# An encoder layer in one program: where the gelu projections, the first recurrence product and the normalisation of the probabilities stand in the order of work

## What is computed

```python
proj = x @ w_in + b_in
u_lru, g_lru, q, k, v, gate_lru, gate_attn = split(proj)
u = depthwise_conv(u_lru)                       # 4 taps, 1280 channels
h = scan(u, forward gates) + scan(u, backward gates)
    # r, i = sigmoid(block_diag(u) + b);  a = exp(8 r log_sigmoid(lam));  h_t = a h_{t-1} + sqrt(1-a^2) i u
y_lru  = (h * gelu(g_lru)) @ w_lru_out
y_attn = windowed_gqa(q, k, v) @ w_attn_out     # 8 heads, 2 KV heads, blocks of 128, +-128 keys, a sink logit
mix = (sigmoid(gate_lru) * y_lru + sigmoid(gate_attn) * y_attn) @ w_o + b_o
x = layer_norm(alpha * x + mix)
hu = depthwise_conv(x @ w_up + b_up)            # 3 taps
val, gt = split(hu)
out = layer_norm(alpha * x + (gelu(gt) * val) @ w_down + b_down)
```

## Time and profile before

| | us |
|---|---|
| median of 3 runs | 2766.47 (2766.07 to 2767.06) |
| the profiled execution, its own time | 2770.9 |
| its span, first to last instruction | 2769.1 |
| PE busy | 2671.8 (96%) |
| DVE / ACT / POOL busy | 1506.4 / 753.4 / 654.1 |
| long sequence: recurrence, attention, merge | 11 to 331, 331 to 741, 741 to 1039 |
| short sequence: recurrence, attention, merge | 1834 to 1998, 1998 to 2201, 2201 to 2356 |

### The profile page before, as it was taken

How to read it: one execution, slowest core, us unless ns; L and a number is a source line. 1 busy time by engine, 2 the same in 40 slices (tenths; PEclk the granted TensorE clock), 3 DMA queues, 4 the chain that set the end, 5 groups by cost and what they waited for, 6 DMA issues and landing times.

```text
span 2769.1 us, 32046 instructions
## 1 busy us (share of the span) xinstructions
PE 2671.8 (96%) x11898; PEld 2202.5 (80%) x11898; DVE 1506.4 (54%) x1800; ACT 753.4 (27%) x1033; POOL 654.1 (24%) x332
## 2 busy tenths in 40 slices
PE   8997999999899999999999999989999999999998
PEld 6886788888678877888888888878788778888886
DVE  7899864334313657745445464667742314644445
ACT  4565713313210022010101011148831211211112
POOL 3554531231133612334343433310000000000000
PEclk9998999999899999999999999999999999999999
DMA  6565654444686833434343534357756794544554
GB/s 232 183 204 185 213 193 160 172 157 159 262 353 231 301 125 137 137 137 153 136 179 128 188 124 161 132 215 235 244 186 228 256 343 159 205 183 182 192 201 168
DMA packets 174272, 535.67 MB, mean 193 GB/s; under 512 B 13863, under 2 KB 40743, under 8 KB 172112
## 3 DMA queue, kind: packets, MB, share of 16 engines
q1 hardware_dynamic: 116992, 430.94, 43.1%
q10 hardware_dynamic: 57168, 103.21, 10.5%
HBM read 310.99 MB, written 214.19 MB: 190 GB/s over the span
## 4 chain that ended last, share of the span: by engine, by line
PE 82%; DVE 9%; DMA 4%; ACT 2%; issue 1%; POOL 1%; ACTq 0%; SPq 0%; DVEq 0%; POOLq 0%
PE ps L857 48%; PE ps L1176 12%; PE ps L1003 8%; PE ps L1097 4%; PE ps L907 3%; PE ps L1036 2%; PE ps L986 2%; DMA gate_in<-gate_dram 1%; DMA W<-w_split 1%; PE ps L1023 1%; PE ps L910 1%; PE ps L1165 1%; DVE tau L1750 1%; DMA al_dram<-AOL 0%; DMA w_split<-W 0%
## 5 line engine op out<-in xcount | busy, mean ns | idle before, releaser
L857 PE MATMUL ps<-XH,W 128*128 128x512 f32 x4224 | 1208.2, 392 | 24.9 <-DVE XL L1695 11.6
L857 PEld LDWEIGHTS ps<-XH,W 128*128 128x128 f32 x4224 | 798.0, 189 | 202.1 <-issue 18.4
L857 PE MATMUL ps<-XL,W 128*128 128x512 f32 x2112 | 712.1, 391 | 0.0
L857 PEld LDWEIGHTS ps<-XL,W 128*128 128x128 f32 x2112 | 399.2, 189 | 83.1
L1176 PE MATMUL ps<-W,HH 128*128 128x512 f32 x1152 | 310.4, 389 | 1.7 <-DVE HL L2006 1.5
L1176 PEld LDWEIGHTS ps<-W,HH 128*128 128x128 f32 x1152 | 216.1, 188 | 47.3 <-DVE HL L2006 1.9
L741 POOL TENSOR_SCALAR W<-raw 128x1024 fp32r<-128x1024 f32 (+2 forms) x72 | 95.4, 1325 | 587.2 <-PE ps L857 277.6
L1003 PE MATMUL ps<-XH,W 128*128 128x512 f32 x672 | 216.4, 393 | 0.0
L807 POOL TENSOR_SCALAR W<-raw 128x1024 fp32r<-128x1024 f32 x72 | 87.4, 1213 | 535.3 <-PE ps L857 224.9
L742 POOL TENSOR_TENSOR W<-raw,W 128x1024 fp32r<-128x1024 f32 (+2 forms) x72 | 200.5, 2785 | 6.0
L808 POOL TENSOR_TENSOR W<-raw,W 128x1024 fp32r<-128x1024 f32 x72 | 191.9, 2666 | 6.0
(11 more groups left out here) (203 smaller groups left out, 3360.6 us busy)
## 6 DMA issues: line engine op xcount, KB each, us to landing
w_split<-W SPq DMA_DIRECT2D x131, 1024.0 KB, 6.4
W<-w_split SPq DMA_DIRECT2D x130, 1024.0 KB, 6.9
raw<-w_mlp SPq DMA_DIRECT2D x72, 512.0 KB, 4.9
raw<-w_qkv_mix SPq DMA_DIRECT2D x28, 512.0 KB, 3.9
w_split<-W SPq DMA_DIRECT2D x8, 1280.0 KB, 12.0
W<-w_split SPq DMA_DIRECT2D x8, 1280.0 KB, 7.7
gate_dram<-mix_out ACTq DMA_DIRECT2D x16, 512.0 KB, 2.7
gate_in<-gate_dram ACTq DMA_DIRECT2D x16, 512.0 KB, 6.2
```

Source lines behind the costliest of these rows:

```text
L857: last = nc.tensor.matmul(bank(group, c), lhs(wl, k), rhs(xl, k, c), start=(k == 0 and n == 0), stop=(k == nk - 1 and n == 2))
```

## The change

It has four parts.

1. **The gelu projections of the second half.** `order_lru` puts `g(1,1)` ahead of gate block (1,1), `g(1,2)` ahead of (1,2) and `g(1,3)` ahead of (1,3). The table `taken_behind` keeps ACT's order as it was, apart from `g(1,0)`, which ACT takes between its two squares of block (1,0). The numbers p of the projections, and so their PSUM groups, are the same.
2. **SP's order at gate slabs (q = 0).** The load of a gate slab stands ahead of the moves of the block before; at (h, 1) `stack_second` and a save too.
3. **The first recurrence product as a fill.** Output 0 of the `w_lru_out` product goes to banks 2-3 and is issued in pieces in the last blocks of kv = 1 (`Y_FILL`): contraction tiles 0-1, 2-4, 5-7 for the long sequence, 0-3, 4-7 for the short. Output 1 follows whole, in banks 4-5. `YR` is loaded by SP for both sequences; gates 0 and 1 are loaded at the start of kv = 1 and their sigmoids are ahead of ACT's wait for the attention's stores. Buffers are laid out anew for it.
4. **Normalisation.** DVE runs `normalise(n+1)` in `tails_of(n)`, ahead of its subtraction on the block's output; DVE no longer waits at the end of the long sequence's attention.

```diff
-                     ("gates", 1, 0), ("g", 1, 0), ("u", 1, 2),
-                     ("gates", 1, 1), ("g", 1, 1), ("u", 1, 3),
-                     ("gates", 1, 2), ("g", 1, 2), ("g", 1, REST_TILE),
-                     ("gates", 1, 3), ("g", 1, 3)]
+                     ("gates", 1, 0), ("g", 1, 0), ("u", 1, 2), ("g", 1, 1),
+                     ("gates", 1, 1), ("u", 1, 3), ("g", 1, 2),
+                     ("gates", 1, 2), ("g", 1, REST_TILE), ("g", 1, 3),
+                     ("gates", 1, 3)]
+        taken_behind = {(0, 0): (("g", 0, 0), ("u", 0, 2), ("g", 0, REST_TILE)), (0, 1): (("g", 0, 1), ("u", 0, 3)),
+                        (0, 2): (("g", 0, 2), ("u", 1, 0)), (1, 0): (("u", 1, 2),),
+                        (1, 1): (("g", 1, 1), ("u", 1, 3)), (1, 2): (("g", 1, 2), ("g", 1, REST_TILE))}
...
+        def lru_group(m):
+
+            return (1, 2)[m] if m < 2 else m % 2
+
+        Y_FILL = ({(6, 1): range(0, 2), (7, 0): range(2, 5), (7, 1): range(5, 8)},
+                  {(3, 0): range(0, 4), (3, 1): range(4, 8)})
...
                 for n, (kind, h, jj) in enumerate(order_lru):
-                    if kind == "gates" and jj:
-                        moves_of_block(0, T, h, jj - 1)
                     if kind == "gates":
                         load(n, n % 2, A["w_gate"][HALF * h + jj, :, :], GATEW)
...
+                    if kind == "gates" and jj > 1:
+                        moves_of_block(0, T, h, jj - 1)
+                    if kind == "gates" and jj == 1:
+                        stack_second(0, T, h)
...
+                    if kind == "gates" and jj == 1:
+                        moves_of_block(0, T, h, 0)
...
-                    if q:
-                        for dst, src in zip(YR[q], (yh_dram, yl_dram)):
-                            sp.dma_start(dst[:, :, 0:T].bitcast(F32), src[q][BLOCKS:RT, :, :].rearrange("k p t -> p k t")).then_inc(y_in[4][q], 16)
+                    if q == 0:
+                        sp.wait_ge(scores_full[q], GROUP * (T // P) * KV)
+                    for dst, src in zip(YR[q], (yh_dram, yl_dram)):
+                        sp.dma_start(dst[:, :, 0:T].bitcast(F32), src[q][BLOCKS:RT, :, :].rearrange("k p t -> p k t")).then_inc(y_in[4][q], 16)
...
+                    def y_fill(n, side):
+
+                        part = Y_FILL[q].get((n, side))
+                        if part is None or kv == 0:
+                            return
+                        if part.start == 0:
+                            pe.wait_ge(mix_taken[q], KD * 2)
+                            slab_in(q, "y_lru", 0)
+                        y_product(0, part)
...
                             mixture_gates(n, 0)
+                            y_fill(n, 0)
                             if n + 1 < nb:
                                 scores(n + 1, (2, 3))
                             turn(n)
                             mixture_gates(n, 1)
+                            y_fill(n, 1)
                             mix_values(n)
...
-                    for m in range(2):
-                        slab_in(q, "y_lru", m)
-                        y_product(m, range(BLOCKS))
-                    for m in range(2):
-                        y_product(m, range(BLOCKS, RT)).then_inc(slab_done, 1)
-                    for m in range(2, KD):
-                        pe.wait_ge(prod_taken[q], m + 1)
+                    y_product(0, range(filled, RT)).then_inc(slab_done, 1)
+                    for m in range(1, KD):
+                        if m == 1:
+                            pe.wait_ge(pt_split[q], KV * pt_before(nb, nb))
+                        elif m == 2:
+                            pe.wait_ge(scores_out[q], GROUP * nb * KV)
+                        else:
+                            pe.wait_ge(prod_taken[q], m + (0 if m == 3 else 1))
                         slab_in(q, "y_lru", m)
                         y_product(m, range(RT)).then_inc(slab_done, 1)
...
+                            if d:
+                                between()
...
+                            decays(h, jj, [side(r, jj, T) for r in sig[0:2]],
+                                   (lambda: take("g", 1, 0)) if (h, jj) == (1, 0) else (lambda: None))
...
-                                for e in behind_gates(h, jj):
+                                for e in taken_behind[h, jj]:
                                     take(*e)
...
-                        if q and kv:
-
+                        if kv:
+
+                            if q == 0:
+                                act.wait_ge(qkv_split[q], 5 * KV)
                             for m in range(2):
                                 act.wait_ge(mix_stored[m][q], 16)
                                 load_gate(m)
...
+                    sigmoid(0)
+                    sigmoid(1)
                     for k in range(3):
                         act.wait_ge(ao_stored[k][q], 32 * ((KV * nb - k + 2) // 3))
...
+                            if n + 1 < nb:
+                                normalise(n + 1)
                             dve.wait_ge(ao_head[q], blk + 1)
...
-                    end_phase(dve, end_of(q, "attn"))
+                    end_phase(dve, end_of(q, "attn"), wait=q > 0)
```

More of the change, by code:

```diff
@@ L274, in build @@
         for k in range(6):
-            part(turn + 64 * 1024 + k * 8192 if k < 2 else at_h + (k - 2) * 8192)
+            part(at_h + k * 8192)
             wo[0].append(place(f"wo{k}", [P, 2, D_MODEL], F32R))
@@ L509, in feature_tile @@
             return BLOCKS + h if jj == REST_TILE else HALF * h + jj
-        def behind_gates(h, jj):
-            at = slab_at[("gates", h, jj)] + 1
-            out = []
-            while at < len(order_lru) and order_lru[at][0] != "gates":
-                out.append(order_lru[at])
-                at += 1
-            return out
         phases = ["lru", "attn", "mlp"]
@@ L940, in _, with y_rhs, y_ready_of, y_product @@
                     per_block = 2 // len(chunks(T))
+                    def y_rhs(t, kk, c):
+                        if kk < BLOCKS:
+                            return x_rhs(t, kk, c)
+                        return YR[q][t][:, kk - BLOCKS, c * CH:(c + 1) * CH]
+                    def y_ready_of(kk):
+                        if kk % 2 == 0:
+                            pe.wait_ge(y_in[kk // 2][q], 64 if kk < BLOCKS else 32)
+                    def y_product(m, part):
+                        return product(lru_group(m), T, RT, slab_lhs(slot_of(q, "y_lru", m)), y_rhs, y_ready_of, part)
+                    def y_fill(n, side):
[6 more added lines that the diff above has]
+                        y_product(0, part)
+                    filled = max(part.stop for part in Y_FILL[q].values())
                     for kv in range(KV):
@@ L1505, in _, with sigmoid @@
                         store(nb - 1)
+                    def sigmoid(i):
+                        act.wait_ge(gate_loaded[i % 2][q], 16 * (i // 2 + 1))
+                        A1(gate_in[q][i % 2][:, 0:T], gate_in[q][i % 2][:, 0:T], ACT.Sigmoid).then_inc(gate_ready[q], 1)
+                    sigmoid(0)
+                    sigmoid(1)
                     for k in range(3):
```

56 lines of the change are left out of this document (19 added, 37 removed).

## The result

The changed kernel takes 2795.57 us (median of 4 runs, 2794.46 to 2796.43) where the kernel before takes 2766.76 (2766.07 to 2767.79): a ratio of 1.0103, with a 95% interval from 1.0091 to 1.0115. It is 28.8 us slower. The forecast was 2769.3, the range 2749 to 2783. The profiled executions differ by less, 2794.5 - 2769.1 = 25.4 us of span, because the one of before was 4.1 above its median and the other 0.9.

A forecast was written before the change was run, and what follows sets the result against it. PE, busy 96% of the span, was taken as the bound, with only 97 us idle and lost clock winnable. Terms -2.2 + 6.2 + 13.6 - 10.8 - 4 = +2.8 us gave 2769.3 us, range 2749 to 2783.

The forecast's parts named there:

- Part 2, -2.2: Long recurrence: SP's earlier gate load removes 1.1 us POOL waits at (0,2) and (0,3), 2.2 us faster; bounds -2.2 and 0.
- PE's next gate block is far enough behind to cover it: Long recurrence, block (0,1): moves come some 4 us later than before, but PE would not be delayed.
- Part 1, long sequence, +6.2: Long recurrence: the 10.9 us won are given back in waits and clock losses, 6.2 us slower; bounds -1.0 and +8.
- The three waits for the gelu: Long recurrence: PE waits for ACT ahead of g(1,2), g(1,3) and the second attention product; steps give 3.5, 3.5, 6.3 us.
- a chain on DVE that the change leaves alone: Long recurrence: scans of block (1,0) still done at 246.4, so ACT's first sigmoid of block (1,1) is done at 248.9.
- Part 1, short sequence, +13.6: Short recurrence: half the product time, almost the same ACT time, so waits for gelus and lost clock; 13.6 us slower.
- Long attention and merge, -10.8: Long merge: YR lands about 747.8, output 2 starts at 764.1 instead of 773.07; 10.8 us faster, bounds -13 and -7.
- Short attention and merge, -4: Short merge: seven outputs end at 2260.1 instead of 2266.0, one gate may be late; 4 us faster, between -7 and +1.
- rival 1: Short attention's end: last mix_values waits for tile 7's landing, stores and gates come 9 us later; 2780.8 us, chance 0.15.
- The price of 7.7 us for a gate load: Short merge: gates come one after another behind attention loads, 7.7 us for the first; one may still be late.
- Rival 2: Both merges: 24 long and 12 short matmuls behind landings run at half clock, +7 us, 2776.5 us; chance 0.13.
- A flat price of 1.8 us for every wait of 2 us or more: PE throughout: each wait of about 2 us or more also costs 1.8 us of lost clock.

The follow-up runs named there:

- E3: Kernel before plus only SP's new order, gate slab loads ahead of the moves: 2768.40 us, ratio 1.0005.
- E12: E8 plus gate loads ahead of the moves for blocks (h,2) and (h,3) only: 2757.59 us, ratio 0.9968.
- E8: Kernel before plus fills in the long sequence alone, early gates and normalising ahead: 2761.02 us, ratio 0.9980.
- E2: Kernel before plus only the gelu projections put ahead of their gate blocks: 2790.60 us, ratio 1.0085.
- E5: Changed kernel without POOL's splits of the slabs of g(1,1), gate block (1,1) and u(1,3), long sequence; trace only: 2782.31 us, one execution.
- E6: Changed kernel without the fills of the short sequence: 2792.25 us, ratio 1.0093.
- E10: Kernel before plus only DVE's normalising ahead: 2768.33 us, ratio 1.0007.
- E11: E8 without normalising ahead, so the kernel before plus fills in the long sequence alone: 2759.85 us, ratio 0.9977.
- E4: Kernel before plus fills in both sequences, early gates and normalising ahead: 2764.14 us, ratio 0.9990.
- E7: Changed kernel, but ACT takes g(1,1) to g(1,3) between the squares of their blocks: 2769.77 us, ratio 1.0011.
- E9: E8 plus gelu projections ahead of their gate blocks and E7's order on ACT: 2762.65 us, ratio 0.9985.

## Why the prediction was wrong

The forecast was 2.8 us slower and it became 28.8, 12.6 beyond the upper end of the range; 0.38 stood on slower. By the terms of its sum:

- **Part 2, -2.2, is the first step that failed.** The sentence "PE's next gate block is far enough behind to cover it" looked for the wrong waiter. ACT stood 8.3 us for the moves of (0,1), its gelu came late, and PE's next product, not its next gate block, waited 1.06 us for the group. What the load ahead won was gone by there: `u(1,1)` starts 0.4 us earlier than before, not 2.2. E3 shows the sum: all of part 2 is worth nothing. That its four other places are worth something by themselves (E12, 3.4 us under E8) is not clear of the noise.
- **Part 1, long sequence, +6.2.** The three waits for the gelu were right to a tenth of a microsecond (3.5, 3.5 and 6.3). The step that failed is "a chain on DVE that the change leaves alone". The change leaves its instructions alone, not its durations: `g(1,1)` ahead of its block (part 1) and SP's earlier load (part 2) both bring POOL's splits beside the scans, and the scans end 5.3 us later. Part 1 alone makes 3.7 of it (E2), part 2 alone 1.8 (E3). The third output started at 254.25 for 248.9, behind a wait of 10.73 us where the forecast's steps leave about 5. E5 shows the cause. With the 2.2 us that part 2 did not pass on and 1.2 us more of clock at the last wait that makes the difference, 13.2 for 4.0, up to about 0.5 us.
- **Part 1, short sequence, +13.6.** Right in its mechanism: from a block's end to the gelu it was 10.1 and 12.9 us, as taken from the earlier trace rows. The term that was too small is the clock. The product `g(1,1)` waited 2.69 us, not 1.4, and in the profiled execution the clock fell there and at every wait behind it: what followed the waits of 2.69, 4.50, 4.69 and 7.40 us took 1.8, 2.9, 1.6 and 2.9 us more than at 2.4 GHz, 9.2 for the forecast's 5.4. 18.2 was measured. In E2 and E6 the same stretch took 14.1 and 14.8 more than before, close to the forecast.
- **Long attention and merge, -10.8.** Right: `YR` was there at 760.6 and output 2 began at 777.0, 12.8 and 12.9 us behind the forecast's 747.8 and 764.1 in a stretch that began 13.2 late, and the stretch is 10.9 shorter. But it was credited to "parts 3 and 4". E10 and E11 show no share of part 4 in it.
- **Short attention and merge, -4.** Wrong, and rival 1 had the mechanism: `mix_values` of the last block waits for tiles that land late, and ACT's last stores and the gates behind them are late with it. None of the 4 us were won. +4.5 stands in the trace and some 3 in the medians of two pairs of kernels, which the scatter of this stretch does not confirm as a size. The forecast gave it 0.15. The price of 7.7 us for a gate load was in hand; what it says, that each gate's load waits its turn in a chain which begins at ACT's phase end, was not followed further than one load.
- **Rival 2, the fills at half clock,** did not come. Here are windows of the changed kernel (stretch, us, busy time of PE, PEld, DVE, ACT, POOL, the granted clock, DMA share, GB/s): the first and the last piece of the fills, which do not wait, the last six matmuls of the piece between them, which stand behind 3.8 us, and the product behind the 7.40 us in the short sequence.

```profile
737.00:742.00 5.00, 5.00 (x25) 4.14 (x23) 2.67 (x6) 3.02 (x11) 0.00 (x0) 0.98 1.04 406
...
749.00:752.00 3.00, 2.69 (x6) 2.05 (x7) 0.00 (x0) 0.00 (x0) 0.00 (x0) 0.50 1.04 406
753.00:758.00 5.00, 5.00 (x23) 4.27 (x22) 1.39 (x2) 1.19 (x2) 0.00 (x0) 0.87 1.05 412
...
2025.00:2029.00 4.00, 3.85 (x9) 3.11 (x10) 3.83 (x6) 3.89 (x6) 0.00 (x0) 0.50 0.00 0
```

In the earlier trace rows the same place stood at 0.50. With the fills PE is at 2.4 GHz for most of the stretch, and only what stands behind a landing of its own begins at 1.2. (That the fills are what keeps the clock up is not shown: E10 has none and stands at 1.00 from 731 to 741 us.) The Trainium skill, page "TensorE: Matmul & The Clock Gate", section "HAM oscillation — how this bites in real kernels", warns of work cut into tiles with a wait ahead of each; here only one of the three pieces waits, ahead of its last tile, and for that tile the rule held.

The parts do not add up exactly. E2, E3 and E4 against before give +23.3, +1.1 and -3.1, together 21.3, where the change gives 28.8. About 3 us of the rest is the meeting of parts 1 and 2 in block (1,1) (first score +13.2 together, +10.1 and +0.4 apart). The other 5 are no larger than the scatter of the runs, above all of E2's, and stay open.

## What to carry to other kernels

Before work is moved into an engine's idle time, ask who sets the end of the stretch. Here it was the chain of scans on DVE: with POOL's split out of the way PE stood 16.7 us for ACT's sigmoid behind that chain (E3), so its 15 us of idle time were the chain's shadow, and moving products into it only moved the wait (E7, E9). When an operation is put earlier, give its consumers' side the same look: a product moved ahead needs its group emptied ahead, and the change of ACT's order that does that was worth 26 us (E7). And where two engines exclude one another, as POOL and DVE do here, a product or a load that comes earlier can bring work of the one beside a chain of the other that the change never touches.

## What the runs showed of the hardware that was not expected

DVE's standstill behind POOL, 2.1 us for one scan, is the first. The second is that a wait of 2 to 3 us decides nothing for certain about the clock. The changed kernel and E6 are the same program up to here; both have PE wait for the same gelu, 2.69 and 2.64 us. These are the windows behind that wait, first in the changed kernel:

```profile
1955.00:1958.00 3.00, 3.00 (x9) 2.39 (x10) 1.21 (x2) 2.97 (x5) 0.00 (x0) 0.63 0.93 332
1958.00:1962.00 4.00, 4.00 (x17) 3.20 (x16) 3.86 (x5) 1.86 (x2) 0.00 (x0) 0.85 0.50 201
```

And in E6:

```profile
1956.00:1959.00 3.00, 3.00 (x13) 2.46 (x14) 1.18 (x2) 2.97 (x5) 0.00 (x0) 1.00 0.97 317
1959.00:1963.00 4.00, 4.00 (x20) 3.28 (x19) 3.86 (x5) 2.15 (x3) 0.00 (x0) 1.00 0.55 223
```

In one the clock fell to 1.2 GHz for part of the stretch, in the other it stayed at 2.4, and the next wait for a gelu was 4.50 in the one (with another fall behind it) and 2.94 in the other, behind 1.46 for DVE. The recurrence of the short sequence took 3.4 us more in the first. A flat price of 1.8 us for every wait of 2 us or more was too simple: in these two kernels a short product behind 2.6 to 2.9 us took 0.2 or 1.8 more than its 5.45, what followed the 7.40 us took 2.9 more in the changed kernel and 1.9 in E6, and what followed the 6.34 took 3.0 more. Such turns may be part of why the medians of two kernels agree less well than their traces; that was not tried.
